# Attention stage of a hybrid decoder step in a new order of units, with two banks for the next pair's products

## The reference, cut to what matters

```python
h = rmsnorm(x); z = h @ w_in                       # q, k, v of attention; q, k, v, gate of mLSTM
q, k = partial_rope(rmsnorm(q)), partial_rope(rmsnorm(k))
# three windows (128, 1), (512, 4), (2048, 16), merged by their softmax denominators
o_a = combine_by_denominators([dilated_band_stats(q, k, v, w, d) for (w, d) in DILATED_PATTERNS])
h_b = mlstm(...)                                   # second stage of the mixer
x += concat(rmsnorm(o_a), gate * rmsnorm(h_b)) @ w_out
x += conv_glu(x); x += per_layer_embed(x)
```

## Time and profile before

| | us |
|---|---|
| median of 3 runs | 3331.43 (3330.22 to 3331.56) |
| profiled execution, its span | 3333.0 |
| PE busy | 3175.4 (95%) |
| DVE busy | 1937.9 (58%) |
| ACT busy | 1021.5 (31%) |
| POOL busy | 627.1 (19%) |

### The profile page before, as it was taken

How to read it: one execution, slowest core, us unless ns; L and a number is a source line. 1 busy time by engine, 2 the same in 40 slices (tenths; PEclk the granted TensorE clock), 3 DMA queues, 4 the chain that set the end, 5 groups by cost and what they waited for, 6 DMA issues and landing times.

```text
span 3333.0 us, 49527 instructions
## 1 busy us (share of the span) xinstructions
PE 3175.4 (95%) x19573; PEld 2878.6 (86%) x19573; DVE 1937.9 (58%) x4392; ACT 1021.5 (31%) x2075; POOL 627.1 (19%) x564
## 2 busy tenths in 40 slices
PE   7899999889999999999999898998999999999999
PEld 6777677579999999999987776774999999999998
DVE  5666454675555555557456654557665555555663
ACT  5333334534111112115333333444331111111241
POOL 2001111212231122211210110113032122212220
PEclk8999999899999999999999999998999999999999
DMA  5121123441111111110221211226221111111111
GB/s 161 45 55 45 45 72 75 148 123 51 44 58 51 39 39 64 39 51 20 91 60 43 54 45 43 71 80 200 52 77 49 41 39 64 39 51 39 39 36 69
DMA packets 209679, 208.78 MB, mean 63 GB/s; under 512 B 36484, under 2 KB 182852, under 8 KB 207344
## 3 DMA queue, kind: packets, MB, share of 16 engines
q1 hardware_dynamic: 209448, 205.62, 20.5%
HBM read 173.96 MB, written 31.61 MB: 62 GB/s over the span
## 4 chain that ended last, share of the span: by engine, by line
PE 84%; DVE 10%; ACT 3%; issue 3%; DMA 0%; DVEq 0%; SPq 0%; ACTq 0%
PE ps L847 25%; PE ps L849 24%; PE ps L848 24%; PE ps L989 2%; PE ps L960 2%; PE ps L975 1%; DVE lo L1753 1%; DVE wb L2270 1%; PE ps L1099 1%; PE ps L1177 1%; DVE acc L1748 1%; ACT zt L1422 1%; PE ps L1180 1%; DVE att L1895 1%; PE ps L1082 0%
## 5 line engine op out<-in xcount | busy, mean ns | idle before, releaser
L806 POOL TENSOR_TENSOR wlo<-raw,whi 128x512 fp32r<-128x512 f32 (+3 forms) x488 | 594.8, 1253 | 2165.5 <-ACT whi L1360 2165.5
L847 PE MATMUL ps<-hi,wlo 128*128 128x344 f32 x2880 | 927.6, 322 | 5.8 <-DVE lo L2192 4.1
L849 PE MATMUL ps<-hi,whi 128*128 128x344 f32 x2880 | 922.5, 320 | 0.0
L848 PE MATMUL ps<-lo,whi 128*128 128x344 f32 x2880 | 921.7, 320 | 0.0
L847 PEld LDWEIGHTS ps<-hi,wlo 128*128 128x128 f32 x2880 | 544.1, 189 | 8.4 <-DVE lo L2192 4.8
L849 PEld LDWEIGHTS ps<-hi,whi 128*128 128x128 f32 x2880 | 543.4, 189 | 0.0
L848 PEld LDWEIGHTS ps<-lo,whi 128*128 128x128 f32 x2880 | 542.3, 188 | 0.6
L847 PE MATMUL ps<-whi,lo 128*128 128x512 f32 (+5 forms) x1152 | 450.5, 391 | 18.0 <-ACT zt L1422 17.2
L849 PE MATMUL ps<-whi,hi 128*128 128x512 f32 (+5 forms) x1152 | 427.7, 371 | 0.0
L848 PE MATMUL ps<-wlo,hi 128*128 128x512 f32 (+5 forms) x1152 | 426.5, 370 | 0.0
L2283 DVE TENSOR_TENSOR X<-X,ps 128x344 f32<-128x344 f32 x528 | 268.1, 512 | 187.8 <-PE ps L849 186.2
(11 more groups left out here) (293 smaller groups left out, 3982.7 us busy)
## 6 DMA issues: line engine op xcount, KB each, us to landing
raw<-in_w_up SPq DMA_DIRECT2D x44, 1024.0 KB, 5.1
raw<-in_w_in SPq DMA_DIRECT2D x112, 256.0 KB, 4.6
raw<-in_w_down SPq DMA_DIRECT2D x22, 1024.0 KB, 4.9
kvb<-in_cache_win_k SPq DMA_DIRECT2D x48, 256.0 KB, 3.2
x_scratch<-X SPq DMA_DIRECT2D x8, 1032.0 KB, 4.9
X<-x_scratch SPq DMA_DIRECT2D x4, 2064.0 KB, 12.6
raw<-in_w_out SPq DMA_DIRECT2D x8, 1024.0 KB, 9.1
raw<-in_w_ple_gate SPq DMA_DIRECT2D x8, 1024.0 KB, 5.0
```

The lines of the kernel that those rows point to most:

```text
L806: pool.tensor_tensor(out=wlo[:, s, r], in0=raw[:, s, r], in1=whi[:, s, r].bitcast(F32), op=ALU.subtract).then_inc(w_split, 1)
L847: nc.tensor.matmul(out, a_lo, b_hi, start=first, stop=False)
L848: nc.tensor.matmul(out, a_hi, b_lo, start=False, stop=False)
L849: return nc.tensor.matmul(out, a_hi, b_hi, start=False, stop=last)
```

## The change

The new `FILL` takes four groups from unit 5 and gives two each to units 14 and 15. Norm and turn parts move to other units; of pair 0's second third, squares and scale now lie ahead of the units. Tiles 1 and 3 of the products go to bank 5, so they wait for other events (`z_before`). The two roundings in the units become four halves at units 3, 4, 5 and 7. At the layer's start the first third is turned around tile 8 of the products. After pair 3's last unit the first tile of pair 5 is made around the last `values`, and eight groups fewer are left beside the gate scans.

```diff
--- before.py
+++ after.py
@@ -141,7 +141,7 @@
 
 
 
-FILL = (8, 8, 8, 4, 4, 8, 4, 4, 4, 4, 4, 4, 4, 4, 0, 0)
+FILL = (8, 8, 8, 4, 4, 4, 4, 4, 4, 4, 4, 4, 4, 4, 2, 2)
 
 
 def ahead(u):
@@ -151,25 +151,27 @@
 
 def norm_part(p, u):
 
-    if u < (6 if p == 0 else 3):
-        return (0, 1 + u // 3, u % 3) if p == 0 else (p, 2, u)
+    if p == 0 and u == 0:
+        return 0, 1, 2
+    if 1 <= u < 4:
+        return p, 2, u - 1
     if p + 1 < PAIRS:
-        for x, a in enumerate((6, 9) if p == 0 else (3, 8)):
+        for x, a in enumerate((4, 9)):
             if a <= u < a + 3:
-                return (p + 1, x, u - a)
+                return p + 1, x, u - a
     return None
 
 
 def turn_part(p, u):
 
-    if p == 0 and u in (3, 4, 6, 7):
-        return (0, u // 3, u % 3)
-    if p and u in (4, 5):
-        return (p, 2, u - 4)
+    if p == 0 and u in (2, 3):
+        return 0, 1, u - 2
+    if u in (6, 7):
+        return p, 2, u - 6
     if p + 1 < PAIRS:
-        for x, a in enumerate((9, 12) if p == 0 else (7, 12)):
+        for x, a in enumerate((8, 12)):
             if u in (a, a + 1):
-                return (p + 1, x, u - a)
+                return p + 1, x, u - a
     return None
 
 
@@ -192,9 +194,22 @@
 
 def z_bank(p, t):
 
+    if p == 0:
+        return (7, 6, 3, 4)[t % 4]
     if p <= PAIRS:
-        return (7, 6, 3, 4)[t % 4] if p == 0 else 7
-    return 7 - (p * (NT + 1) + t) % 2
+        return 5 if t in (1, 3) else 7
+    return 7 - (p * (NT + 1) + t + 1) % 2
+
+
+def z_before(p, t):
+
+    i = p * (NT + 1) + t
+    if p <= PAIRS:
+        return i - 1 if t in (2, 3, 4) else i
+    return i if (p, t) == (PAIRS + 1, 0) else i - 1
+
+
+ROUND = {3: (0, 0), 4: (0, 1), 5: (1, 0), 7: (1, 1)}
 
 
 def y_bank(t):
@@ -900,7 +915,10 @@
                         t, k = divmod(n, KT)
                         i = p * (NT + 1) + t
                         if k == 0 and p:
-                            pe.wait_ge(*at(z_done, i if p <= PAIRS else i - 1))
+                            if 1 <= p <= PAIRS and t == 1:
+                                pe.wait_ge(*at(pt1, far(NU * (p - 1))))
+                            else:
+                                pe.wait_ge(*at(z_done, z_before(p, t)))
                         elif k == 0 and t >= 4:
                             pe.wait_ge(*at(z_done, t - 3))
                         elif k == 0 and l == 0 and t == 3:
@@ -997,16 +1015,19 @@
 
 
                 pe.wait_ge(*at(tl_done, 0))
-                for t in range(NT + 1):
+                for t in range(NT):
                     products(0, KT * t, KT * (t + 1))
                     if t == 1:
                         pe.wait_ge(*at(ple_done, 0))
                         column_sums()
                 pe.wait_ge(*at(rcol_done, 1))
 
-                pe.wait_ge(*at(z_done, NT + 1))
-                for j in range(2):
-                    turn_third(0, 0, j)
+                pe.wait_ge(*at(z_done, 6))
+                turn_third(0, 0, 0)
+                products(0, KT * NT, KT * NT + 4)
+                turn_third(0, 0, 1)
+                products(0, KT * NT + 4, NPROD)
+                pe.wait_ge(*at(z_done, NT))
                 scores(0, 0)
                 pe.wait_ge(*at(k_evac, 1))
                 for p in range(PAIRS):
@@ -1044,7 +1065,9 @@
                             if part:
                                 pe.wait_ge(*at(o_read, NT * p + qb))
                                 turn_third(*part)
+                products(PAIRS + 1, 0, 4)
                 values(PAIRS - 1, NT - 1)
+                products(PAIRS + 1, 4, KT)
                 turn_back(PAIRS - 1, NT - 1)
 
                 def gate_rows():
@@ -1120,7 +1143,7 @@
                         pe.wait_ge(*at(pt1, far(NU * PAIRS)))
                         pe.wait_ge(*at(o_read, NT * PAIRS))
                         gate_rows()
-                        next_products(0, EARLY)
+                        next_products(KT, EARLY)
                         gate_columns()
 
                         pe.wait_ge(*at(em_done, 1))
@@ -1359,6 +1382,13 @@
                     scale_block(g, 0, KT)
                 do(nc.scalar.activation(whi[:, s, 0:used], raw[:, s, 0:used], ACT.Copy), w_hi, wait=False)
 
+            def round_half(g, half):
+
+                s, n = g % NSLOT, BLOCKS[g % NBLK][3] // 2
+                act.wait_ge(raw_in[s], raw_value(g))
+                r = slice(half * n, (half + 1) * n)
+                do(nc.scalar.activation(whi[:, s, r], raw[:, s, r], ACT.Copy), w_hi if half else None, wait=(half == 0))
+
             def square(at, i, n, l=1):
                 c, k = squares_order(i, l)[n]
                 sem, value = at(sq_used, 24 * i + n - 1)
@@ -1477,7 +1507,9 @@
                     z_evac(0, t)
                     if t == 4:
                         head_root(0, 0)
-                evac_third(0, 0)
+                    elif t == NT - 1:
+                        evac_third(0, 0)
+                head_root(0, 1)
                 probabilities(0, 0)
                 for p in range(PAIRS):
                     for u in range(NU):
@@ -1496,8 +1528,8 @@
                         part = norm_part(p, u)
                         if part and part[2] == 0:
                             head_root(part[0], part[1])
-                        if u in (3, 5):
-                            round_block(B + 2 * (p + 2) + u // 5)
+                        if u in ROUND:
+                            round_half(B + 2 * (p + 2) + ROUND[u][0], ROUND[u][1])
                         if p == 0 and u == 9:
                             act.wait_ge(*at(gz_abs, 1))
                             do(nc.scalar.activation(gt[:, :, :], gt[:, :, :], ACT.Exp, scale=-1.0))
@@ -1820,6 +1852,13 @@
                     do(v.tensor_tensor(out=zr[:, :, :, RH:], in0=tmp[0][:, :, :, RH:], in1=tmp[1][:, :, :, 0:RH], op=ALU.add),
                        qk_norm)
 
+                def evac_third(p, x):
+
+                    dve.wait_ge(*at(turned, 2 * (3 * p + x) + 2))
+                    k3 = qkA[p % 2][1][:, third(x), :]
+                    src = ps[:, 6, 0:k3.shape[1] * P].rearrange("p (t n) -> p t n", n=P)
+                    do(v.tensor_copy(k3, src), k_evac, wait=False)
+
                 dve.wait_ge(const_in, 16 * (1 + 5 * DEPTH))
 
                 s9, t9 = yrs[:, 0:NT + 1], yt2[:, 0:NT + 1]
@@ -1843,16 +1882,13 @@
                                               in1=bgate[0:m, l, :], op0=ALU.mult, op1=ALU.add), gates_read)
                     if 4 <= t < 7:
                         (norm_squares, norm_scale, norm_rope)[t - 4](0, 0)
+                    elif t == NT - 1:
+                        norm_squares(0, 1)
+                        evac_third(0, 0)
+                norm_scale(0, 1)
                 f = gz[:, :, NH:2 * NH]
                 do(v.scalar_tensor_tensor(out=gt[:, :, :], in0=f, scalar=-1.0, in1=f, op0=ALU.mult, op1=ALU.max), gz_abs)
                 do(v.tensor_scalar(f, f, 0.0, None, ALU.min))
-
-                def evac_third(p, x):
-
-                    dve.wait_ge(*at(turned, 2 * (3 * p + x) + 2))
-                    k3 = qkA[p % 2][1][:, third(x), :]
-                    src = ps[:, 6, 0:k3.shape[1] * P].rearrange("p (t n) -> p t n", n=P)
-                    do(v.tensor_copy(k3, src), k_evac, wait=False)
 
                 def evac_k(p):
                     for half in range(2):
```

## The result

The changed kernel takes 3299.08 us in the median of four runs (3296.84 to 3303.09), the kernel before 3330.82 beside it: a ratio of 0.9907, 95% interval 0.9895 to 0.9919. The forecast was 3300.6. The profiled execution has a span of 3298.6 against 3333.0.

A forecast was written before the change was run, and what follows sets the result against it. PE carries 84% of the span, so time is gained only where it stands still or runs at the lower clock. Layers gain 15.2 and 15.6 us, 30.8 off 3333.0; taken to the runs' median, 3300.6 us, range 3275 to 3320.

The forecast's parts named there:

- Start of the stage: Layer's start: thirds turned around tile 8 let pair 1's first product begin near 86.4; 4.0 us less per layer.
- Two banks and even fill: Pair units: 8.4 us of tile waits nearly all go, as do far and near copy waits of 4.5 and 2.5.
- The meeting in unit 7: DVE's small scale operations take 0.93 us beside POOL's split; scores wait 2.35 in pairs 0 and 1, 3.6 in pair 2.
- clock stretch: PE running at half clock for 3.3 us behind a long wait; priced at 1.45 us each.
- Rival 3: Unit 7: scale begins before the split or slips between pieces; three waits and clock stretches go, 25.3 us; 3275, chance 0.12.
- Other small waits 0.2: Sum by pair: allowance of 0.2 us for all waits not priced separately.
- The forecast for pair 3 up to unit 14's values: Pair 3 to its unit 14: waits with clock fall from 5.2 to 0.1, 5.1 us less per layer.
- End of the stage: Behind pair 3: less cover for DVE's scans, PE stands 4.4 us; +3.1 in layer 0, +4.3 in layer 1.
- Rival 2: Units 6 and 8: query copies stay late behind half roundings and `values` waits again; +58 us, 3359, chance 0.06.
- ACT comes free sooner: Halved roundings and later turns free ACT about 0.8 us before needed; `values` waits of 2.5 and 2.9 us go.
- Rival 1: Units 7 and 9: new waits 0.5 longer and one more per pair reaching a clock stretch; +12 us, 3312, chance 0.12.
- Rival 4: Whole stage: waits only move on and start's gain cancels end's loss; within 5 us of 3331, chance 0.08.

The follow-up runs named there:

- e5: Changed kernel with all product tiles of a pair in one bank (7) again, bank 5 unused; 3310.41 us.
- e6: Changed kernel with the old groups per unit: 8 in unit 5, none in units 14 and 15; 3304.36 us.
- e1: Changed kernel with the four half roundings at units 6, 7, 12 and 13 in place of 3, 4, 5 and 7; 3280.38 us.
- e7: Changed kernel with each split by POOL in 8 pieces of half the columns in place of 4; 3278.83 us.
- e9: Changed kernel with norms and turns of pairs 1 to 3 at the units of the kernel before, roundings still halved; 3296.04 us.
- e2: Changed kernel with the norm of the next pair's second third at units 8 to 10 in place of 9 to 11; 3293.04 us.
- e3: Changed kernel without products around pair 3's last values; all 18 groups stand beside the gate scans; 3290.55 us.
- e4: Changed kernel with two whole roundings at units 3 and 5 in place of four halves; 3317.27 us.
- e8: Changed kernel with two whole roundings at units 6 and 12 in place of four halves; 3298.21 us.
- c2: Changed kernel with the edits of e1, e2, e3 and an earlier query norm, plus one group ahead of the last values and one behind; 3257.41 us.
- c3: Changed kernel with the edits of e1, e2, e3, an earlier query norm and splits in 8 pieces; 3247.85 us.

## Why the prediction was right, and where its steps were not

**Start of the stage.** The first product of pair 1 was forecast near 86.4 and began at 86.25. Pair 0 lost 6.2 and 7.4 us where 5.9 (1.6 of clock and 4.3) and 7.5 (1.6 and 5.9) were forecast. This step was right.

**Two banks and even fill.** The tile waits went, 8.4 to 0.2 us in layer 0. e5 puts 11.3 us of the median on the bank, of which 8.5 are idle time of PE in the two stages. The waits on the far and near copies, 4.5 and 2.5 us a layer, went as forecast, but by e6 the even fill as a whole is worth 1.8 us of stage beside the meeting in unit 7, since it takes cover from that wait.

**The meeting in unit 7.** Forecast 2.35, 2.35 and 3.6 us with DVE's small operations at 0.93; measured 2.22, 2.26 and 3.53 with 0.92 to 0.94, and a clock stretch behind each. Two terms of the working were a little off and did not matter: the first of the four operations took 0.40, and PE's share adds up to 4.0 us, not to 4.1. e1 and e7 change just this step: without the meeting 24 us of stage go, and with half the piece the operations take 0.52. Rival 3 did not come by itself; e1 brings it about, and takes 18.7 us off the median where that rival had 25 off the forecast. The Trainium skill's page SBUF — State Buffer, section "SBUF: two separate sides", has GpSimd, and DVE where it reads two SBUF inputs or runs in a 2-port mode, take their shared ports as an exclusive lock for a whole instruction. The traces agree: an operation of 0.17 us takes nearly as long as one piece, 0.93 us at 384 columns and 0.52 at 192. The prediction drew from the rule that a scale ahead of the split would push POOL back and the scores would not wait. e9 shows part of that in pair 1: the four small operations were over before the split began at 186.94, and the scores of unit 7 waited 0.48 us in place of 2.26. Only the wide operation met the split; both took longer there, it 1.68 us and the split 4.63 in place of 3.91.

**Missed: the turn in unit 12.** "Other small waits 0.2" left this wait at nothing, without a reason. `turn_part` has the second third in units 12 and 13, `norm_part` its rope in unit 11, and DVE comes to that rope only behind the near copy: 1.7 us in each of pairs 0 to 2, 10.4 in all, and 14.3 of stage when they are taken away (e2). The wait was to be had from the diff: the same list put the first third's rope at 6 and its turn at 8, the second's at 11 and 12. It was to be had from the kernel before as well, whose pair 0 already had its rope in unit 11 and its turn in unit 12. Timeline of DVE, then of PE, before:

```profile
154.13 0.26 DVE L1820 TENSOR_TENSOR zt<-rowr 128x96 f32<-128x96 f32 x1
...
154.49 0.52 PE L934 MATMUL ps<-ident,zt 128*128 128x128 f32 x3 [1.39 <-issue]
```

The change kept this placement in pair 0 and brought it to pairs 1 and 2.

**What made up for it.** The forecast for pair 3 up to unit 14's values was 5.1 us; it was 82.9 before (325.2 to 408.06) and 75.2 after (312.3 to 387.52), 7.6 less. About 1.4 of that (two groups of 0.70) are the fill that moved behind those values, which the working had not credited. The traces say of what kind the whole gain is. In the two stages PE's idle time fell by 17.7 us (59.8 to 42.1), the time at the lower clock from 34 to 24 us, which is 5 us at half rate, and the remaining 8.2 us of the 30.9 are a shorter busy time of PE for the same matmuls. The forecast had no term for that. In pair 1, for example, idle time fell by 1.95 us where the forecast's waits come to 3.3 less, and busy time by 0.96 with the same clock stretch. With the old fill (e6) 4.7 us of the busy time are back, so a good part belongs to the fill. Why a busy time shrinks is argued, not shown: ends of matmuls are modelled, so that "idle before" may show less of a short wait than taking it away gives back. The sum was right partly by luck, because this and the missed wait nearly cancel.

**End of the stage.** From the values of unit 14 to the first gate column it was 24.55 us before and 26.6 after, 2.05 more where 1.7 was forecast; the wait at L1085 was 4.29 where 4.4 was; the clock behind it was at 0.50. e3 takes the products away and gets 3.3 to 3.4 us a layer back. This part did speak against the change, as forecast.

**Rivals.** Rival 2, late query copies, did not come: no wait of `values` on a query third is left. e9 shows its mechanism alive at the old units, 2.0 and 2.2 us where it was 2.5 and 2.9. The reason that the prediction gave for the halves, that ACT comes free sooner, is the step that fell: at the new units e4 and e8 with whole roundings have at most 0.4 us of such waits, and lose 18 us each, one against the changed kernel and one against e1, because the splits start at other times. So the later turns cleared the query copies; the halves are worth at most 0.5 and 0.7 us a wait at the old units, and at the new ones they only placed the splits. Rival 1 did not come either: no scores of unit 9 wait, and those of unit 7 wait no longer than forecast. Rival 4 is out by the measured gain of 31.7 us.

## What to carry to other kernels

Where two engines exclude one another for an instruction, look in the timeline for the moments at which a long series of the one meets a series of short operations of the other on a path that somebody waits for, and place the releasing step by the microsecond at which it ends, not by its unit. Shorter pieces on the background engine are a cheap cure where moving is hard. Products filled in ahead of a fixed chain of another engine are paid for at its end, save as many as fill a wait that is there anyway (c2); those that stand beside it are free.

## What was not expected of the hardware

- An operation of 12 elements on DVE takes nearly as long as one of POOL's pieces beside it: 0.17 us alone, 0.52 beside pieces of 192 columns, 0.93 beside 384. `masked` and the copies, which read PSUM, were not lengthened beside the same splits: `masked` of 384 columns took 0.56 us beside one in e4 and 0.56 with none in the changed kernel.
- POOL pays for small pieces: eight of 192 columns took 5.19 us beside DVE, four of 384 took 3.91, and PE's waits for `wlo` grew from 0.4 to 3.7 us. Even so the program gained 20 us by them (e7), and was 9 us faster with them on top of all else (c3).
- The clock's price is not fixed. Behind waits of 2.2 us it stood at 0.50 for 3.3 us (after, pair 1), for about 6.6 (e5, layer 0) and not at all (e5, layer 1); in e4 a wait of 3.48 us in pair 0 was followed by a low stretch in layer 0 and by none in layer 1. Behind the waits of 1.7 us in unit 12 no low stretch was seen in the changed kernel. So a forecast of 1.45 us for each long wait can hold in the mean only.
- Outside the stage one and the same program part took 2639.5 to 2648.7 us in the eleven changed kernels with four pieces, with the clock at its lower level for 113 to 137 us of it. Medians a few microseconds apart therefore say little about a single edit here, while the pieces of the stage repeat to 0.2 us between layers wherever the clock does (e1: 70.9, 71.9, 71.9, 101.8 and 70.9, 71.9, 71.9, 101.9).
